# A feed-forward's tail on one Trainium2 core: the second norm of tile zero brought forward, its transposes put between the last products

## The chip, the cores and the metric

The kernel runs on one core of one Trainium2 chip. Five engines work side by side and meet only at semaphores: PE (TensorE, matrix products and transposes), DVE (VectorE), ACT (ScalarE), POOL (GpSimd) and SP (SyncE, which here only starts transfers). PE writes to PSUM, eight banks of 128 rows by 512 fp32 columns. The metric is the device time of one execution in microseconds (us); lower is better. Three runs of the kernel before took 904.01, 907.29 and 907.97 us, so its time is 907.29 us, the median.

## The reference, cut to what matters

Two transformer blocks run one after the other on 256 tokens of width 1024, all in fp32. The first ends with a feed-forward and a layer norm. The second puts 16 learned tokens (meta tokens) in front, norms the 272 rows again and multiplies them by a wide input matrix; mixing, routing and 32 experts follow.

```
h = x * (1.0 + sc2) + sh2
f = square(relu(h @ w_ff1)) @ w_ff2
x = layer_norm(ALPHA * x + gt2 * f, ln2_g, ln2_b)           # end of block one
...
h = layer_norm_2(concat([meta, x]), ln_emb_g, ln_emb_b)     # start of block two
proj = h @ w_in        # dn_qkv, dn_z, dn_b, dn_a, sb_qkv, gates
```

The change is at the seam: two layer norms in a row on the same rows, with the last feed-forward products before them and the first products of `w_in` behind them.

## The kernel before, in words

The 256 tokens are two tiles of 128, tile zero and tile one. `X[:, t, :]` holds a tile with tokens on the partitions; `hT` holds the same values with features on the partitions, as eight slices k of 128 features, which is the form that a product takes as its operand. Going from `X` to `hT` takes eight PE transposes into two PSUM banks (`transposes`, line 2184; banks 0 and 1 for tile zero, 2 and 3 for tile one) and eight evacuations that also apply the gain and the bias of the second norm (`features` on ACT, line 2514; for tile one DVE does four of the eight, `to_hT`, line 2682).

Every engine's program is written out by hand in one fixed order, with waits on semaphores. There is no scheduler: what stands later on an engine waits for what stands earlier.

The second feed-forward product is done in a form with seven products for eight (numbered 1 to 7, each summing 16 steps j in the PSUM bank of its own number; `ff2`, line 2466). The last work of this stage on PE is product 7 for j = 8 to 15 and then product 4 for j = 8 to 15. In the trace each fp32 product is two instructions. Each product raises the semaphore `yh` at j = 15; the fifth gives tile zero its last part, product 7 one half of tile one, and product 4 (`yh` = 9) the other half.

DVE takes the parts up: `ffn_out(t, half, ...)` is four instructions on 512 columns (sum, gate, residual, statistics; lines 2955 to 2958), `ffn_moments` one, `normalise(3, t)` the first norm (reciprocal, lines 2673 and 2675), and `second_norm(t)` the second (two statistics on line 2661, line 2663, a square root by ACT on line 2509, a reciprocal, line 2670). Before the change DVE's order is: tile zero's two halves, its first norm, one half of tile one (with the sum of line 2981), the second norm of tile zero, the other half of tile one, and its two norms. Each norm raises `xn`; `xn_count(i, t)` says how often it must have been raised.

`pe_second` is PE's program for block two. Before the change it begins with the transposes of tile zero, then a product on tile zero's `hT` (the value part of `sb_qkv` for tile zero, line 496, 8 products of 512 columns into bank 6; it waits for `hT0`, which ACT raises after slices 0 to 3 and again after 4 to 7), then the transposes of tile one, then `pe_side(0)`: the first quarter of the product that gives z (line 471, 8 products of 256 columns into bank 7, on tile zero only). The product on line 504 (`dn_b` and `dn_a`, all 272 rows) is the first that needs tile one's `hT`. Behind it line 520 runs 22 groups of products on all rows.

The weights come through a ring of five slots that SP fills; a slot is filled again when PE has raised `used` for what was in it.

Of the kernel before, what the change touches and what calls it, by code (L numbers as in the profile page):

```python
# [15 lines left out]
KD = DM // P  # L16
# [170 lines left out]
def build(nc, IN, out):  # L187

    ctx = ExitStack()
    with ctx:  # L190
# [15 lines left out]
        S = namedtuple("Semaphores", names)(*[ctx.enter_context(nc.semaphore("s_" + n)) for n in names])  # L206
# [22 lines left out]
        def V(name, a=0, b=None):  # L229
            o, k = COLS[name]  # L230
            return col[:, o + a:o + (k if b is None else b)]
# [121 lines left out]
        def xn_count(i, t):  # L353

            return 6 + 2 * t + i - 4 if i in (3, 4) else 2 * (i - 1) + t + 1
# [101 lines left out]
            else:  # L457
                eng.wait_ge(S.g2_mm, side_before + 3 * (i // 4) + i % 4 + 1)

        def pe_side(pe, mm, i):  # L460
            n = AT["dn_z"] + i // 4
            if i % 4 == 0:
                landed_wait(pe, n)
            earlier = [j for j in range(i) if SIDE_BANK[j] == SIDE_BANK[i]]
            if earlier:
                pe.wait_ge(S.side_ev, earlier[-1] + 1)
            w = ring_at(n).rearrange("p (k n) -> p k n", k=KD)
            o = psum[:, SIDE_BANK[i], 0:NT]
            for k in range(KD):
                if i < 4:  # L470
                    last = mm(o, hT[:, k, tok(i // 2)], w[:, k, (i % 2) * NT:(i % 2 + 1) * NT],
                              start=(k == 0), stop=(k == KD - 1))
                else:
                    last = mm(o, w[:, k, (i % 4) * P:(i % 4 + 1) * P], hT[:, k, META:L2],  # L474
                              start=(k == 0), stop=(k == KD - 1))
            last.then_inc(S.used if i % 4 == 3 else S.g2_mm, 1)

        def act_side(act, i):
            side_wait(act, i)
# [7 lines left out]

        def pe_second(pe, mm, transposes, out_proj, keep_warm):
            tr = nc.tensor.transpose
            transposes(4, 0, 1)  # L490
            landed_wait(pe, AT["sb_qkv"] + 2)
            w = ring_at(AT["sb_qkv"] + 2).rearrange("p (k n) -> p k n", k=KD)
            for k in range(KD):
                if k % 4 == 0:
                    pe.wait_ge(S.hT0, k // 4 + 1)
                last = mm(b_(6), hT[:, k, tok(0)], w[:, k, :], start=(k == 0), stop=(k == KD - 1))
            last.then_inc(S.g2_mm, 1)
            transposes(4, 1)
            pe_side(pe, mm, 0)
            pe.wait_ge(S.hT, 4)  # L500

            pe.wait_ge(S.in_dn, 48)
            for k in range(KD):
                last = mm(psum[0:8, 4, 0:L2], wba[:, k, :], hT[:, k, :], start=(k == 0), stop=(k == KD - 1))
            last.then_inc(S.ba_mm, 1)
            for g, (n, m, form) in enumerate(GROUPS):
# [5 lines left out]
                for k in range(KD):  # L512
                    if form == 2:
                        for j in range(4):
                            last = mm(psum[32 * j:32 * j + 32, g % 4, 0:P].rearrange("p (a d) -> p a d", a=2),
                                      hT[:, k, 0:32],
                                      w[:, k, :].rearrange("p (a h d) -> p a h d", a=2, h=4)[:, :, j, :],
                                      start=(k == 0), stop=(k == KD - 1))
                    elif form == "T":
                        last = mm(psum[:, g % 4, 0:L2], w[:, k, m * P:(m + 1) * P], hT[:, k, :],  # L520
                                  start=(k == 0), stop=(k == KD - 1))
                    else:
                        last = mm(psum[:, g % 4, :], hT[:, k, tok(form)], w[:, k, :],
                                  start=(k == 0), stop=(k == KD - 1))
                last.then_inc(S.used if ends_chunk(g) else S.g2_mm, 1)
                if g == 0:
                    pe.wait_ge(S.ba_ev, 1)
                    for t in range(3):
                        last = tr(psum[0:(META if t == 2 else P), 5, 8 * t:8 * t + 8], baT[:, tok(t)],
                                  C("ident")[0:8, 0:8])  # L530
# [22 lines left out]
            for t, b in enumerate((3, 7, 4)):  # L553
# [4 lines left out]
                for h in range(DH):  # L558
                    last = tr(psum[0:(META if t == 2 else P), b, h * P:(h + 1) * P], cv[:, 8 + h, tok(t)], C("ident"))
# [3 lines left out]
            for t in range(3):  # L563
                for h in range(DH):
                    last = tr(psum[0:(META if t == 2 else P), t, h * P:(h + 1) * P], cv[:, 4 + h, tok(t)], C("ident"))
# [19 lines left out]
            for p in range(12):  # L585
                last = tr(bank_prob(0, p, 2), prob(M2, p), C("ident") if p < 8 else C("ident")[0:META, 0:META])
# [52 lines left out]
            for h in range(DH):  # L639
                last = mm(psum[0:META, 5, h * P:(h + 1) * P], prob(M6, 8 + h), vb[0:META, 2, h * P:(h + 1) * P],  # L640
                          start=True, stop=True)
# [6 lines left out]
            for p in range(8):  # L648
                last = mm(psum[LOW, 3, 64 * p:64 * p + 64], prob(M4, p)[LOW, LOW], prob(M5, p)[LOW, LOW],
                          start=True, stop=True)  # L650
            last.then_inc(S.rd_mm, 1)
            pe.wait_ge(S.uv, 1)
            for h in range(DH):
                last = mm(psum[:, 2, h * P:(h + 1) * P], kdec[0:META, 2, h * P:(h + 1) * P],
                          M2[0:META, h * P:(h + 1) * P], start=True, stop=True)
# [4 lines left out]
            for p in range(8):  # L660
                last = mm(psum[LOW, 4, 64 * p:64 * p + 64], prob(M3, p)[HIGH, LOW], prob(M6, p)[HIGH, HIGH],
                          start=True, stop=True)
# [5 lines left out]
            for p in range(8):  # L668
                f = slice(64 * p, 64 * p + 64)
                last = mm(psum[LOW, 3, f], T1n[:, f], Yc[:, f], start=True, stop=True)  # L670
# [116 lines left out]
            for h in range(DH):  # L787
                last = mm(psum[:, 0, h * P:(h + 1) * P], kdec[:, 0, h * P:(h + 1) * P], M4[:, h * P:(h + 1) * P],
                          start=True, stop=True)
# [1375 lines left out]
        def _(pe):  # L2165
# [282 lines left out]
            def ff2(j, products):  # L2448

                n = ff2_chunk(j // 2)
                landed_wait(pe, n)
                pe.wait_ge(S.ff_st, j + 1)
                w = ring_at(n).rearrange("p (m n) -> p m n", m=4)
                a = [fTr[:, (2 * j + k) % 16, :] for k in range(2)]
                b = [w[:, 2 * (j % 2) + k, :] for k in range(2)]
                S1, S2, S3, S4 = SK[:, j % 2, 0, :], SK[:, j % 2, 1, :], SK3[:, j % 8, :], SK[:, j % 2, 2, :]  # L2460
                T1, T2, T3, T4 = TWK[j % 2][0], TWK[j % 2][1], TK[:, j % 8, 0, :], TK[:, j % 8, 1, :]
                for i in products:
                    lhsT, rhs = {1: (a[0][:, 0:P], b[0][:, 0:512]), 2: (a[1][:, 0:P], b[1][:, 0:512]),
                                 3: (S4, b[1][:, 512:DM]), 4: (a[1][:, P:NT], T4),
                                 5: (S1, T1), 6: (S2, T2), 7: (S3, T3)}[i]
                    last = mm(b_(i), lhsT, rhs, start=(j == 0), stop=(j == FT // 2 - 1))  # L2466
                    if j == FT // 2 - 1:
                        last.then_inc(S.yh, 1)
                return last
# [19 lines left out]
            ff2(15, (1, 6, 5, 3, 2))  # L2489
            for i in (7, 4):  # L2490
                for j in range(8, 16):
                    last = ff2(j, (i,))
                    if i == 7 and j == 8:
                        last.then_inc(S.used, 1)
# [4 lines left out]
        def _(act):  # L2499
# [7 lines left out]
            def ln_sqrt(i, t):  # L2507
                act.wait_ge(S.ln_v, ln_count(i, t))
                nc.scalar.activation(sd[:, t:t + 1], mv[:, t, 1:2], ACT.Sqrt, bias=epsc).then_inc(S.ln_s, 1)

            def features(i, t, ks, A1, B1):
                act.wait_ge(S.xn_tr, tr_count(i, t))
                for k in ks:
                    last = nc.scalar.activation(hT[:, k, tok(t)],
                                                psum[:, 2 * t + k // 4, (k % 4) * P:(k % 4 + 1) * P],
                                                ACT.Identity, bias=B1[:, k:k + 1], scale=A1[:, k:k + 1])
                return last
# [119 lines left out]
            ln_sqrt(3, 0)  # L2637
            ln_sqrt(4, 0)
            features(3, 0, range(4), V("ge"), V("be")).then_inc(S.hT0, 1)
            ln_sqrt(3, 1)  # L2640
            features(3, 0, range(4, KD), V("ge"), V("be")).then_inc(S.hT0, 1)
            ln_sqrt(4, 1)
            features(3, 1, range(4, KD), V("ge"), V("be")).then_inc(S.hT, 1)
            act_second(act, link, ln_sqrt, act_hT)
# [3 lines left out]
        def _(dve):  # L2648
# [16 lines left out]
            def normalise(i, t, rows=None):  # L2665

                dve.wait_ge(S.ln_s, ln_count(i, t))
                link(v.reciprocal(rstd[:, t:t + 1], sd[:, t:t + 1]))
                if rows is None:
                    v.tensor_scalar(X[:, t, :], X[:, t, :], mv[:, t, 0:1], rstd[:, t:t + 1],  # L2670
                                    ALU.subtract, ALU.mult).then_inc(S.xn, 1)
                else:
                    link(v.scalar_tensor_tensor(X[:, t, :], X[:, t, :], mv[:, t, 0:1], rows[:, 0, :],
                                                ALU.subtract, ALU.mult))
                    v.scalar_tensor_tensor(X[:, t, :], X[:, t, :], rstd[:, t:t + 1], rows[:, 1, :],
                                           ALU.mult, ALU.add).then_inc(S.xn, 1)
# [286 lines left out]
            def second_norm(t):  # L2963
                dve.wait_ge(S.xn, xn_count(3, t))
                moments(4, t)
                normalise(4, t)
# [10 lines left out]
            link(ffn_out(0, 0, p1s, 2))  # L2977
            ffn_moments(0)
            normalise(3, 0, rowB[:, 0])
            dve.wait_ge(S.yh, 8)  # L2980
            v.tensor_tensor(u3s, u2s, b_(7), ALU.add)
            ffn_out(1, 1, vs, 7)
            second_norm(0)
            dve.wait_ge(S.yh, 9)
            link(ffn_out(1, 0, u3s, 4))
            ffn_moments(1)
# [104 lines left out]
```

## Time and profile before

| | |
|---|---|
| runs (median, lowest, highest) | 907.29, 904.01, 907.97 us |
| profiled execution | 907.25 us |
| its span, from first to last instruction | 905.4 us |
| mean granted TensorE clock | 0.989 of full speed |
| PE busy | 867.8 us (96% of the span) |
| DVE, ACT, POOL busy | 361.7, 180.5, 93.1 us |
| the stretch of the change | 348 to 381 us |

Rows of the trace are instructions of one engine that were merged where they follow each other: start, duration of the row, engine, line, operation, output <- inputs, count, and in square brackets how long the engine had been idle before and what ended that. PE's instructions overlap in its pipeline, so a row's duration is a little longer than the time after which the next can start; the rows of the chain of waits (the work that ended last, followed back) have that overlap taken off. PEclk is the clock that was granted to TensorE, as a share of full speed.

### The profile page before, as it was taken

Reading aid. Unit: us, or ns where it says so; the run is one execution under the profiler, and the core shown is the slowest. Engines: PE = TensorE matmul, PEld = TensorE weight load, DVE = VectorE, ACT = ScalarE, POOL = GpSimd, SP = SyncE. Lnnn points to the kernel's source line nnn. Section 1 sums busy time; section 2 is a strip of 40 time slices with the busy share of each in tenths; the row PEclk is TensorE's granted clock in tenths of the full one; section 3 lists DMA queues with packets and bytes.
Section 4 is the critical chain, followed back from the end, with each engine's and each line's share of the span. In section 5 each row is a group of like instructions: output and inputs, shape, how many; then the busy total and the mean of one; then the engine's idle time right before and its main releaser. Section 6 shows DMA issues by size and latency. Waiting matters only on the chain.

```text
span 905.4 us, 11803 instructions
## 1 busy us (share of the span) xinstructions
PE 867.8 (96%) x4825; PEld 546.4 (60%) x4825; DVE 361.7 (40%) x826; ACT 180.5 (20%) x368; POOL 93.1 (10%) x91
## 2 busy tenths in 40 slices
PE   6999899999999999899999999999989999999994
PEld 3446757766667774588868888877455333333331
DVE  5735846533223338465094523533264111101014
ACT  4126512100000000322323224530111111001001
POOL 0034242401011110300000000000200000000000
PEclk9999999999999999999999999999989999999998
DMA  9997776643334446024343222024969999999993
GB/s 366 429 420 285 295 310 245 266 186 147 123 128 172 185 187 266 1 93 143 136 168 112 95 94 94 9 93 146 427 263 321 372 402 425 419 422 422 418 416 139
DMA packets 24653, 218.29 MB, mean 241 GB/s; under 512 B 3658, under 2 KB 3938, under 8 KB 10003
## 3 DMA queue, kind: packets, MB, share of 16 engines
q1 hardware_dynamic: 21330, 205.76, 57.0%
q0 software_dynamic: 3264, 11.72, 3.5%
q8 instruction: 40, 0.66, 0.3%
q14 instruction: 19, 0.15, 0.0%
HBM read 218.65 MB, written 2.10 MB: 244 GB/s over the span
## 4 chain that ended last, share of the span: by engine, by line
PE 90%; DVE 5%; ACT 2%; issue 1%; DMA 1%; SPq 0%; DVEq 0%; ACTq 0%
PE psum L2444 12%; PE psum L2466 9%; PE psum L1462 9%; PE psum L520 8%; PE psum L474 6%; PE psum L2225 6%; PE psum L1517 4%; PE psum L1486 4%; PE psum L803 3%; PE psum L2417 3%; PE psum L2199 3%; PE psum L2170 3%; PE psum L597 2%; PE psum L1440 1%; DMA ring<-in_stream 1%
## 5 line engine op out<-in xcount | busy, mean ns | idle before, releaser
L2444 PE MATMUL psum<-hT,ring 128*128 128x256 f32 x512 | 115.3, 379 | 0.0
L2444 PEld LDWEIGHTS psum<-hT,ring 128*128 128x128 f32 x512 | 97.1, 190 | 24.8 <-issue 13.1
L520 PE MATMUL psum<-hT,ring 128*128 128x272 f32 x320 | 74.2, 393 | 0.0
L520 PEld LDWEIGHTS psum<-hT,ring 128*128 128x128 f32 x320 | 60.6, 190 | 12.9 <-issue 0.5
L2466 PE MATMUL psum<-scr 128*128 128x512 f32 x128 | 59.5, 592 | 0.0
L2928 DVE TENSOR_TENSOR scr<-ring 128x512 f32<-128x512 f32 x16 | 11.1, 691 | 119.4 <-PE psum L2466 119.4
L474 PE MATMUL psum<-hT,ring 128*128 128x256 f32 x256 | 58.6, 383 | 0.0
L1462 PE MATMUL psum<-ring,hT 128*32 128x512 f32 (+1 forms) x240 | 56.5, 594 | 0.1
L2225 PE MATMUL psum<-ring,hT 128*128 128x512 f32 (+1 forms) x128 | 54.2, 586 | 2.1 <-ACT hT L2538 2.1
L1462 PE MATMUL psum<-scr,hT 128*64 128x512 f32 (+1 forms) x192 | 51.6, 614 | 2.2 <-issue 2.2
L1871 DVE TENSOR_TENSOR scr<-psum,scr 128x256 f32<-128x256 f32 x11 | 4.7, 425 | 119.6 <-ACT scr L1631 119.6
L474 PEld LDWEIGHTS psum<-hT,ring 128*128 128x128 f32 x256 | 47.5, 190 | 7.0 <-issue 0.6
L2466 PE MATMUL psum<-ring,scr 128*128 128x512 f32 x96 | 46.2, 592 | 0.0
L2633 ACT ACTIVATE scr<-psum 128x256 f32<-128x256 f32 x32 | 12.3, 383 | 168.7 <-PE psum L2444 168.7
L2225 PEld LDWEIGHTS psum<-ring,hT 128*128 128x128 f32 x128 | 24.9, 195 | 31.0 <-issue 31.0
L2466 PEld LDWEIGHTS psum<-scr 128*128 128x128 f32 x128 | 24.3, 190 | 24.6 <-issue 23.9
L2158 POOL TENSOR_TENSOR scr<-scr 128x256 f32<-128x256 f32 x32 | 20.6, 644 | 154.5 <-ACT scr L2633 154.5
L1486 PE MATMUL psum<-rowB,scr 128*128 128x512 f32 x80 | 36.3, 596 | 0.0
L2170 PE MATMUL psum<-cst 128*128 128x512 f32 x66 | 31.7, 627 | 0.0
L1462 PEld LDWEIGHTS psum<-ring,hT 128*32 128x32 f32 (+1 forms) x240 | 16.1, 119 | 23.1 <-issue 22.4
L803 PE MATMUL psum<-scr,ring 128*128 128x256 f32 x128 | 29.0, 382 | 0.0
L1462 PEld LDWEIGHTS psum<-scr,hT 128*64 128x64 f32 (+1 forms) x192 | 14.7, 129 | 23.2 <-issue 23.2
(579 smaller groups left out, 1271.3 us busy)
## 6 DMA issues: line engine op xcount, KB each, us to landing
ring<-in_stream SPq DMA_DIRECT2D x54, 2048.0 KB, 9.4
ring<-in_gates SPq DMA_DIRECT2D x9, 2048.0 KB, 21.6
ring<-in_downs SPq DMA_DIRECT2D x14, 1024.0 KB, 21.8
scr<-in_gates SPq DMA_DIRECT2D x6, 2048.0 KB, 26.8
scr<-in_gates SPq DMA_DIRECT2D x8, 1024.0 KB, 29.0
scr<-in_downs SPq DMA_DIRECT2D x8, 1024.0 KB, 15.4
scr<-in_stream SPq DMA_DIRECT2D x3, 2048.0 KB, 19.1
rowB<-in_rows POOLq DMA_DIRECT2D x5, 1024.0 KB, 12.1
```

Source lines behind the costliest of these rows:

```text
L474: last = mm(o, w[:, k, (i % 4) * P:(i % 4 + 1) * P], hT[:, k, META:L2], start=(k == 0), stop=(k == KD - 1))
L520: last = mm(psum[:, g % 4, 0:L2], w[:, k, m * P:(m + 1) * P], hT[:, k, :], start=(k == 0), stop=(k == KD - 1))
L803: last = mm(o, w[:, k, m * P:(m + 1) * P], src[:, k, :], start=(k == 0), stop=(k == 3))
L1462: last = mm(psum[i * w:(i + 1) * w, 2, :], xg[p % 2][:, k, i * w:(i + 1) * w], block_of(GATE[e], k), start=(k == 0), stop=(k == KD - 1))
L1486: last = mm(b_(4 + 2 * t + half), scat[p % 2][:, t * P:(t + 1) * P], yg[:, half * 512:(half + 1) * 512], start=(p == 0), stop=False)
L1517: last = mm(psum[i * w:(i + 1) * w, half, :], turned[p % 2][:, c:c + w], block_of(DOWN[e], 4 * (e % 2) + 2 * half + f), start=(f == 0), st ...
L2170: mm(psum[:, bank, 0:width], C("ident"), C("neg").broadcast_to([P, width]), start=True, stop=True)
L2199: last = mm(b_(4 + 2 * t + half), src[:, k, t * P:(t + 1) * P], w[:, k, :], start=(k == 0), stop=(k == KD - 1))
L2225: return mm(psum[:, 2 * c + t, 0:b - a], hT[:, k, tok(t)], ring_at(AT["head"] + k)[:, 2048 + a:2048 + b], start=(k == 0), stop=(k == KD - 1))
L2417: last = mm(o, mixT[:, k, t * P:(t + 1) * P], w[:, k, cols], start=(k == 4), stop=(k == 3))
L2444: last = mm(psum[:, f if f < 4 else 0, 0:NT], w[:, k, m * P:(m + 1) * P], hT[:, k, META:L2], start=(k == order[0]), stop=(k == order[-1]))
L2466: last = mm(b_(i), lhsT, rhs, start=(j == 0), stop=(j == FT // 2 - 1))
```

## The change

Four pieces move. On DVE, `second_norm(0)` goes from behind the first half of tile one to directly behind the first norm of tile zero. On PE, `transposes(4, 0, 1)` (tile zero) goes from the head of `pe_second` to in front of product 4's last two steps, j = 14 and 15. On PE, the z quarter is cut in two: slices 0 to 3 before the transposes of tile one, slices 4 to 7 behind them, with a new wait for `xn` (first norm of tile one) ahead of the first half. On ACT, the square root of tile one's first norm goes behind the second four evacuations of tile zero. No instruction is added or removed.

PE at the end of the feed-forward (line numbers in the changed kernel are a few higher: 2468 is 2466, 2186 is 2184). Before:

```order
L2466 MATMUL psum<-scr 128x512 x16
L2184 MATMUL psum<-cst,X 128x128 x8
L496 MATMUL psum<-ring,hT 128x512 x8
L2184 MATMUL psum<-cst,X 128x128 x8
L471 MATMUL psum<-ring,hT 128x256 x8
```

And now:

```order
L2468 MATMUL psum<-scr 128x512 x14
L2186 MATMUL psum<-cst,X 128x128 x8
L2468 MATMUL psum<-scr 128x512 x2
L496 MATMUL psum<-ring,hT 128x512 x8
L471 MATMUL psum<-ring,hT 128x256 x4
L2186 MATMUL psum<-cst,X 128x128 x8
L471 MATMUL psum<-ring,hT 128x256 x4
```

Tile zero's eight transposes now stand ahead of the last two products, and tile one's stand in the middle of the z quarter.

DVE from the last instruction of tile zero's first norm on (2675, now 2679) to the first instruction that needs product 4. Before:

```order
L2675 SCALAR_TENSOR_TENSOR X<-X,small,rowB 128x1024
L2981 TENSOR_TENSOR scr<-scr,psum 128x512
L2955 TENSOR_TENSOR scr<-scr,psum 128x512
L2956 TENSOR_TENSOR scr<-scr 128x512
L2957 SCALAR_TENSOR_TENSOR X<-X,scr 128x512
L2958 BN_STATS small<-X 128x6
L2661 BN_STATS small<-X 128x6 x2
L2663 BN_AGGR small<-small 128x2
L2668 RECIPROCAL small<-small 128x1
L2670 TENSOR_SCALAR X<-X,small 128x1024
L2955 TENSOR_TENSOR scr<-scr,psum 128x512
```

And now:

```order
L2679 SCALAR_TENSOR_TENSOR X<-X,small,rowB 128x1024
L2665 BN_STATS small<-X 128x6 x2
L2667 BN_AGGR small<-small 128x2
L2672 RECIPROCAL small<-small 128x1
L2674 TENSOR_SCALAR X<-X,small 128x1024
L2986 TENSOR_TENSOR scr<-scr,psum 128x512
L2959 TENSOR_TENSOR scr<-scr,psum 128x512
L2960 TENSOR_TENSOR scr<-scr 128x512
L2961 SCALAR_TENSOR_TENSOR X<-X,scr 128x512
L2962 BN_STATS small<-X 128x6
L2959 TENSOR_TENSOR scr<-scr,psum 128x512
```

The four instructions of the second norm have changed places with the five of tile one's first half. The diff:

```
-        def pe_side(pe, mm, i):
+        def pe_side(pe, mm, i, ks=range(KD)):
...
-            for k in range(KD):
+            for k in ks:
                 if i < 4:
                     last = mm(o, hT[:, k, tok(i // 2)], w[:, k, (i % 2) * NT:(i % 2 + 1) * NT],
                               start=(k == 0), stop=(k == KD - 1))
...
-            last.then_inc(S.used if i % 4 == 3 else S.g2_mm, 1)
+            if KD - 1 in ks:
+                last.then_inc(S.used if i % 4 == 3 else S.g2_mm, 1)
...
         def pe_second(pe, mm, transposes, out_proj, keep_warm):
             tr = nc.tensor.transpose
-            transposes(4, 0, 1)
             landed_wait(pe, AT["sb_qkv"] + 2)
...
             last.then_inc(S.g2_mm, 1)
+            pe.wait_ge(S.xn, xn_count(3, 1))
+            pe_side(pe, mm, 0, range(4))
             transposes(4, 1)
-            pe_side(pe, mm, 0)
+            pe_side(pe, mm, 0, range(4, KD))
             pe.wait_ge(S.hT, 4)
...
             for i in (7, 4):
                 for j in range(8, 16):
+                    if i == 4 and j == 14:
+                        transposes(4, 0, 1)
                     last = ff2(j, (i,))
...
             features(3, 0, range(4), V("ge"), V("be")).then_inc(S.hT0, 1)
+            features(3, 0, range(4, KD), V("ge"), V("be")).then_inc(S.hT0, 1)
             ln_sqrt(3, 1)
-            features(3, 0, range(4, KD), V("ge"), V("be")).then_inc(S.hT0, 1)
             ln_sqrt(4, 1)
...
             normalise(3, 0, rowB[:, 0])
+            second_norm(0)
             dve.wait_ge(S.yh, 8)
             v.tensor_tensor(u3s, u2s, b_(7), ALU.add)
             ffn_out(1, 1, vs, 7)
-            second_norm(0)
             dve.wait_ge(S.yh, 9)
```

## Rows read from the trace of the kernel before

**Rows 1.** The page: the span, and each engine's busy time

```profile
span 905.4 us, 11803 instructions
PE 867.8 (96%) x4825; PEld 546.4 (60%) x4825; DVE 361.7 (40%) x826; ACT 180.5 (20%) x368; POOL 93.1 (10%) x91
```

**Rows 2.** Chain of waits in order of time: start, duration, what

```profile
363.18 1.11 PE psum L2184 x8
364.31 1.51 ACT hT L2514 x4
...
373.06 0.87 PE psum L2184 x8
373.93 3.46 PE psum L471 x16
...
385.26 58.86 PE psum L520 x256
```

**Rows 3.** Timeline of PE across the seam

```profile
348.48 13.90 PE L2466 MATMUL psum<-scr 128*128 128x512 f32 x32
...
363.18 1.09 PE L2184 MATMUL psum<-cst,X 128*128 128x128 f32 x8 [0.80 <-DVE X L2670]
...
365.95 7.11 PE L496 MATMUL psum<-ring,hT 128*128 128x512 f32 x16 [1.69 <-ACT hT L2514]
...
377.32 3.83 PE L504 MATMUL psum<-hT,sm 128*8 128x272 f32 x16
```

**Rows 4.** The page's groups: line 2466, busy and mean ns

```profile
L2466 PE MATMUL psum<-scr 128*128 128x512 f32 x128 | 59.5, 592 | 0.0
```

**Rows 5.** Timeline of DVE in the same stretch

```profile
355.65 1.28 DVE L2675 SCALAR_TENSOR_TENSOR X<-X,small,rowB 128x1024 f32<-128x1024 f32 x1
356.86 0.68 DVE L2981 TENSOR_TENSOR scr<-scr,psum 128x512 f32<-128x512 f32 x1
...
360.23 1.27 DVE L2661 BATCH_NORM_STATS2 small<-X 128x6 f32<-128x512 f32 x2
...
362.31 0.81 DVE L2670 TENSOR_SCALAR X<-X,small 128x1024 f32<-128x1024 f32 x1
363.04 0.68 DVE L2955 TENSOR_TENSOR scr<-scr,psum 128x512 f32<-128x512 f32 x1
...
368.02 1.28 DVE L2675 SCALAR_TENSOR_TENSOR X<-X,small,rowB 128x1024 f32<-128x1024 f32 x1
...
371.43 0.81 DVE L2670 TENSOR_SCALAR X<-X,small 128x1024 f32<-128x1024 f32 x1
```

**Rows 6.** Timeline of ACT in the same stretch

```profile
361.78 0.29 ACT L2509 ACTIVATE small<-small 128x1 f32<-128x1 f32 x1 [7.68 <-DVE small L2663]
...
366.17 0.29 ACT L2509 ACTIVATE small<-small 128x1 f32<-128x1 f32 x1 [0.36 <-DVE small L2961]
...
373.97 1.50 ACT L2514 ACTIVATE hT<-psum,col 128x128 f32<-128x128 f32 x4 [2.77 <-PE psum L2184]
...
375.97 1.28 ACT L482 ACT_TABLE_LOAD   x1
```

**Rows 7.** Windows: PE, PEld, DVE, ACT, POOL busy, clock, DMA share, GB/s

```profile
360.00:375.00 15.00, 12.52 (x44) 6.69 (x43) 11.81 (x23) 4.80 (x14) 0.92 (x1) 1.00 0.00 0
...
670.00:680.00 10.00, 9.24 (x33) 6.48 (x34) 5.75 (x30) 0.30 (x2) 0.00 (x0) 0.55 0.18 73
...
720.00:760.00 40.00, 39.98 (x219) 14.89 (x216) 7.02 (x15) 4.40 (x9) 2.97 (x3) 1.00 1.00 407
760.00:800.00 40.00, 37.74 (x195) 14.49 (x195) 5.73 (x11) 5.05 (x9) 1.98 (x2) 0.96 1.02 422
```

**Rows 8.** Waits of SP's transfer queue from 560 us on

```profile
SPq L2010 <- DVE perm L1732: 18.6, 1, 18.6
```

**Rows 9.** Timeline of PE in the experts

```profile
779.67 8.78 PE L1462 MATMUL psum<-scr,hT 128*64 128x512 f32 x32 [2.24 <-issue]
```

**Rows 10.** Chain of waits later on, same line and count

```profile
829.17 7.02 PE psum L1462 x32
```

More of the change, by code:

```diff
@@ L458, in side_wait, with pe_side @@
                 eng.wait_ge(S.g2_mm, side_before + 3 * (i // 4) + i % 4 + 1)
-        def pe_side(pe, mm, i):
+        def pe_side(pe, mm, i, ks=range(KD)):
             n = AT["dn_z"] + i // 4
@@ L468, in pe_side @@
             o = psum[:, SIDE_BANK[i], 0:NT]
-            for k in range(KD):
+            for k in ks:
                 if i < 4:
@@ L475, in pe_side @@
                               start=(k == 0), stop=(k == KD - 1))
-            last.then_inc(S.used if i % 4 == 3 else S.g2_mm, 1)
+            if KD - 1 in ks:
+                last.then_inc(S.used if i % 4 == 3 else S.g2_mm, 1)
         def act_side(act, i):
@@ L489, in pe_second @@
             tr = nc.tensor.transpose
-            transposes(4, 0, 1)
             landed_wait(pe, AT["sb_qkv"] + 2)
@@ L497, in pe_second @@
             last.then_inc(S.g2_mm, 1)
+            pe.wait_ge(S.xn, xn_count(3, 1))
+            pe_side(pe, mm, 0, range(4))
             transposes(4, 1)
-            pe_side(pe, mm, 0)
+            pe_side(pe, mm, 0, range(4, KD))
             pe.wait_ge(S.hT, 4)
@@ L2491, in _ @@
                 for j in range(8, 16):
+                    if i == 4 and j == 14:
+                        transposes(4, 0, 1)
                     last = ff2(j, (i,))
@@ L2639, in _ @@
             features(3, 0, range(4), V("ge"), V("be")).then_inc(S.hT0, 1)
+            features(3, 0, range(4, KD), V("ge"), V("be")).then_inc(S.hT0, 1)
             ln_sqrt(3, 1)
-            features(3, 0, range(4, KD), V("ge"), V("be")).then_inc(S.hT0, 1)
             ln_sqrt(4, 1)
@@ L2979, in _ @@
             normalise(3, 0, rowB[:, 0])
+            second_norm(0)
             dve.wait_ge(S.yh, 8)
@@ L2982, in _ @@
             ffn_out(1, 1, vs, 7)
-            second_norm(0)
             dve.wait_ge(S.yh, 9)
```

## The prediction

> **What bounds the kernel now.** I read the page first: PE is busy 867.8 of 905.4 us [rows 1], so this is a kernel bound by PE, and time can only be won where PE stands idle or works slowly. The chain of waits comes next: across the seam it leaves PE for DVE and ACT and comes back, and behind it runs on PE in one piece, as in the 58.86 us of line 520 [rows 2]. So the seam is a place where PE waits for somebody. The timeline of PE says how long: 0.80 us before the transposes of tile zero (for line 2670, the last step of its second norm) and 1.69 us before line 496 (for ACT's first four evacuations) [rows 3]. Together 2.49 us of 905.4, 0.3%. Timelines of DVE and ACT then say when each operand is ready [rows 5, 6], and the windows that the clock granted here is 1.00 and that no transfer runs [rows 7].
>
> **Step 1: tile zero's second norm.** DVE ends line 2675 at 355.65 + 1.28 = 356.93. Before, five instructions of tile one come first, from 356.86 to 360.23, 3.37 us, and the second norm takes from 360.23 to 362.31 + 0.81 = 363.12, 2.89 us with ACT's square root in it [rows 5]. Moved ahead, it runs from about 356.97 to 359.86. The five instructions follow, until 359.86 + 3.37 = 363.23 less the overlap of about 0.07 that rows 5 show between neighbours (2675 ends at 356.93, 2981 starts at 356.86): about 363.2.
>
> **Step 2: the transposes between the products.** The last 32 instructions of line 2466 take 13.90 us, each lasts 0.592 [rows 3, 4]; so one starts every (13.90 - 0.592) / 31 = 0.429 us. Product 4's j = 14 starts at 348.48 + 28 x 0.429 = 360.50. The operand is there at 359.86, so the transposes wait for nothing, with 0.64 us to spare. Eight of them take 0.87 us net [rows 2], and push j = 14 and 15 back by that: product 4, which ended at 348.48 + 13.90 = 362.38 [rows 3], ends at 363.25. A wait is added in front of these products, so this margin counts: behind it stand four product instructions, and for them DVE's second half of tile one.
>
> The Trainium skill, "TensorE: Matmul & The Clock Gate", section "Back-to-back issue gap", gives some 81 ns for each 128-column matmul in a sustained stream with weight loads; by that figure the eight would take an estimated 0.65 us, and the gain would come out about 0.1 us larger. The trace has 0.87 us, 109 ns each, and the sum goes by that.
>
> **Step 3: line 496.** ACT's four evacuations start when the transposes' last result is there, 1.09 us after their start [rows 3] and about 0.04 later, and take 1.51; PE starts 0.13 behind, as 365.82 to 365.95 [rows 2, 3]: 360.50 + 1.09 + 0.04 + 1.51 + 0.13 = 363.27. PE itself is free at 360.50 + 0.87 + 4 x 0.429 = 363.09. So line 496 starts at 363.27 where it started at 365.95 [rows 3]: 2.68 us earlier. The stall of 1.69 us shrinks to 0.2, because four product instructions, 1.72 us, now lie over ACT's work.
>
> **Step 4: tile one, which is late next.** DVE can take the last part at 363.2 by its own work and at 363.25 + 0.04 by PE's: 363.29 instead of 363.04, 0.25 us later. From there to the end of tile one's second norm DVE needs what it needed, 371.43 + 0.81 - 363.04 = 9.20 us [rows 5], so the operand of tile one's transposes is ready at 372.49 instead of 372.24. ACT's reordering costs nothing: its eight evacuations of tile zero end near 361.6 + 3.0 = 364.6, and the square root that now stands behind them is wanted at about 366.17 + 0.25 [rows 6], so 1.8 us cover it; without that cover it would add 1 for 1.
>
> **Step 5: the z quarter as filler.** Line 496's 16 instructions take 16 x 0.429 = 6.87, until 370.14. The new wait for tile one's first norm is met at 368.02 + 1.28 + 0.25 = 369.55 [rows 5], 0.6 us before. If it were not, nothing is lost but filler: behind it on PE stand half the z quarter and tile one's transposes, and these wait for a later norm anyway. Half of line 471, 3.46 / 2 = 1.73 [rows 2], fills PE until 371.87. Then PE waits for the operand until 372.49 + 0.06 (as 363.12 to 363.18 [rows 3, 5]) = 372.55, 0.68 us idle. Without the cut it would have idled 2.4 us.
>
> **Step 6: where the gain is handed on.** Tile one's transposes start at 372.55. PE goes on with 0.87 + 1.73 until 375.15. ACT and DVE end tile one's `hT` at 372.55 + 1.09 + 0.04 + 1.50 = 375.18 [rows 3, 6], and PE starts line 504 behind it at 375.18 + 0.13 = 375.31. Before it started at 377.32 [rows 3], held by its own queue and not by `hT`, which was ready near 375.47 [rows 6]. The sum is 377.32 - 375.31 = 2.01 us, 2.0. What was a chain on PE (transposes and a whole z quarter behind tile one's norm) has become a chain DVE, PE, ACT; tile one's norm is the next limit, and it did not move.
>
> **Does it reach the end?** Behind line 504 PE works without a hole for 58.86 us and more [rows 2]; ACT's table load and DVE's small work that lie there [rows 6] take their turn from PE's results and move along. No transfer hangs on the moved instructions: none runs from 360 to 375 [rows 7], and the next slots are released by line 520. The experts stream at 407 to 422 GB/s [rows 7] and could hold the end in place, but that stream is started by DVE's routing result (18.6 us of SP's waiting [rows 8]), in a stretch where the DMA share is 0.18 [rows 7]; it moves along too.
>
> **The sum.** The profiled execution took 907.25 us, 905.4 of span and 1.85 around it, and stands 0.04 under the median of the runs, so no correction: 907.25 - 2.0 = 905.25, say 905.3. Bounds: PE without any hole from 360.50 to tile one's transposes (0.87 + 1.72 + 6.87 + 1.73) and 2.76 us of evacuation and restart behind them would start line 504 at 374.45, a gain of 2.9; with the gain lost below, 0.
>
> **The rivals.** (a) The gain is real at the seam and does not reach the end: the experts' weights arrive when they did. For it: the DMA share of 1.00 to 1.02 from 720 to 800 and the 2.24 us that PE waited at 777 us [rows 7, 9]. Against: the released start above. Then 907.0 to 907.3.
>
> (b) Slower: the second norm is not ready when PE reaches its transposes, and the two products behind them stall. The place is product 4, j = 14; each us beyond the margin of 0.64 delays product 4, tile one and line 504 by one. The 2.0 us are used up when the norm ends 2.64 us late, taking 5.5 us where it took 2.89. If it were 4 us late, 907.25 + 1.4 = 908.6. For it: the norm needs ACT in its middle. Against: ACT had been idle for 7.68 us when this square root came to it [rows 6], and DVE has nothing else in between.
>
> (c) The clock elsewhere. The granted clock fell to 0.55 on average from 670 to 680 us and to 0.96 from 760 to 800, the second time around a wait of PE for 2.24 us [rows 7, 9]; these are its two levels, 2.4 and 1.2 GHz, mixed over the window. The second spell cost line 1462 8.78 us where 32 such took 7.02 [rows 9, 10], 1.76 us. One such spell more makes 907.1, one less 903.5; one like the first, up to 4.5 us, makes 909.8 or 900.8. The Trainium skill, the same page, "Part 1: The HAM clock gate", says that the clock is halved by default and that the array's activity releases it; by that rule fewer holes at the seam can win a spell there, but the clock there is 1.00 already [rows 7], so the seam has none to win.
>
> (d) The change does not do what it says: DVE still ends tile one late and PE waits the whole gain away in front of tile one's transposes. That needs tile one's norm 2 us later than 372.49; 0.25 us is all that the rows give. Then 907.3.
>
> **How the numbers follow.** Forecast 0.72, at 905.3; (a) and (d) together 0.16, at 907.0 to 907.3; (b) 0.04, at 908.6; (c) 0.08, half to each side. The runs of before spread from 3.3 below to 0.7 above their median, and a median of a few runs moves by part of that; so the range goes from 905.3 - 2.4 to (a) and 0.6 above it, 902.9 to 907.8. About 0.5% (4.5 us) is what a measurement of this kernel can tell from no change; 2 us is less than half. Faster by more needs 902.75 or less: the spread around the forecast gives 0.05 and a lost spell of clock 0.02, 0.07. Slower by more needs 911.8: (b) and (c) at their worst, 0.03. The rest, 0.90, is no change that can be told.
>
> **What would show it.** The transposes of tile zero start at about 360.5 with no idle time and line 496 near 363.3; the idle time before line 496 falls from 1.69 to 0.2 us; a new wait of about 0.7 us for line 2670 (2674 in the changed kernel) stands before tile one's transposes; line 504 starts 2.0 us earlier, and the start of the transfers behind the routing is earlier by as much. It is wrong if the transposes between the products wait, if tile one's norm ends more than 0.5 us later, or if the 2 us are at line 504 and no longer at the end.

## The result: 902.01 us, and the profile after

The changed kernel took 902.01 us, the median of five runs (901.85 to 902.89), beside 907.29 us for the kernel before (904.01 to 908.66, five runs). The medians differ by 5.3 us; the ratio on record is 0.9948, with a 95% interval of 0.9925 to 0.9970. Forecast were 2.0 us less, and 902.9 was the lower end of the range; to 902.75 or less I had given 0.07. The direction was right, the size was not. Its profiled execution took 901.93 us, with a span of 900.1 us against 905.4 [rows 1] and a granted clock of 0.993 against 0.989.

The timeline of PE across the seam in the changed kernel, to be laid beside [rows 3] (line 2468 is 2466 of before, 2186 is 2184, 506 is 504; in the experiments below the numbers move by a few again, and a row is known by its operation and tiles):

```profile
347.78 12.18 PE L2468 MATMUL psum<-scr 128*128 128x512 f32 x28
359.79 1.04 PE L2186 MATMUL psum<-cst,X 128*128 128x128 f32 x8
360.67 1.88 PE L2468 MATMUL psum<-scr 128*128 128x512 f32 x4
362.52 7.11 PE L496 MATMUL psum<-ring,hT 128*128 128x512 f32 x16
369.46 1.89 PE L471 MATMUL psum<-ring,hT 128*128 128x256 f32 x8
371.86 1.09 PE L2186 MATMUL psum<-cst,X 128*128 128x128 f32 x8 [0.51 <-DVE X L2674]
372.79 1.89 PE L471 MATMUL psum<-ring,hT 128*128 128x256 f32 x8
374.61 3.83 PE L506 MATMUL psum<-hT,sm 128*8 128x272 f32 x16
```

The row of line 2468 starts 0.70 us earlier than in the kernel before (347.78 for 348.48), long before anything that the change touches: that belongs to this execution, not to the change. Counted from there, line 506 starts after 26.83 us and line 504 of before after 28.84. The seam gives 2.01 us. The distance hardly varies: it is 28.83 to 28.85 us in all five traces with the order of before (before, e2, e6, e8 and e13 below) and 26.83 to 26.85 in all six with the order of the change (after, e3, e5, e7, e9, e14). Both idle times of [rows 3] are gone, and one of 0.51 us is new, before tile one's transposes.

The timeline of DVE in the same stretch, beside [rows 5]:

```profile
356.27 1.29 DVE L2665 BATCH_NORM_STATS2 small<-X 128x6 f32<-128x512 f32 x2
...
358.36 0.82 DVE L2674 TENSOR_SCALAR X<-X,small 128x1024 f32<-128x1024 f32 x1
359.09 0.68 DVE L2986 TENSOR_TENSOR scr<-scr,psum 128x512 f32<-128x512 f32 x1
...
362.58 0.69 DVE L2959 TENSOR_TENSOR scr<-scr,psum 128x512 f32<-128x512 f32 x1
...
370.99 0.81 DVE L2674 TENSOR_SCALAR X<-X,small 128x1024 f32<-128x1024 f32 x1
```

Tile zero's second norm ends at 359.18 and PE's transposes start at 359.79: the spare 0.6 us are there.

So where are the other 3 us? I followed the same instructions through both traces. Up to the routing the lead stays what it was at line 506: line 1371 starts 2.72 us earlier. At the first expert product it is 5.82. The timeline of PE there, in the kernel before:

```profile
670.76 0.41 PE L1371 MATMUL psum<-scr,cst 128*128 128x32 f32 x2 [1.78 <-DVE scr L1698]
...
684.01 2.37 PE L1462 MATMUL psum<-ring,hT 128*64 128x512 f32 x10
```

and in the changed kernel (lines two higher):

```profile
668.04 0.41 PE L1373 MATMUL psum<-scr,cst 128*128 128x32 f32 x2 [1.77 <-DVE scr L1700]
...
678.19 2.37 PE L1464 MATMUL psum<-ring,hT 128*64 128x512 f32 x10
```

The same work takes 13.25 us in one and 10.15 in the other. The windows of the changed kernel (columns as in [rows 7]) say why:

```profile
660.00:670.00 10.00, 7.49 (x40) 4.81 (x39) 8.23 (x37) 3.09 (x7) 0.53 (x1) 0.97 0.87 348
670.00:680.00 10.00, 9.91 (x58) 6.44 (x59) 7.43 (x32) 1.87 (x2) 0.43 (x1) 0.86 0.40 134
```

The clock shares missing here, 0.03 and 0.14 of 10 us, make 3.4 us at 1.2 GHz; in the kernel before the share was 0.55 from 670 to 680 [rows 7], and windows of 1 us put its spell from 671.0 to 681.3, 10.2 us. In the experts a little is given back: line 1464 of the seventh group, in front of which the code waits for the group's weights, starts 5.48 us earlier, and it idles 2.69 us for 2.24 [rows 9]:

```profile
774.19 8.79 PE L1464 MATMUL psum<-scr,hT 128*64 128x512 f32 x32 [2.69 <-issue]
```

The account of the profiled pair: 0.70 (earlier work of that execution) + 2.01 (seam) + 3.10 (routing) - 0.34 (before the seventh group) - 0.2 (behind it) = 5.3 us of span. It holds for these two executions; how far it holds for the medians is what the experiments are about.

### The profile page after: what moved, and what is told of

Read it like the earlier page. It is cut to its first block, busy times and chain, and to the rows that moved or that the text cites. A ratio compares the mean times of both kernels' runs of the same rounds, so it can differ in the third digit from the quotient of the medians.

```text
span 900.1 us, 11804 instructions
## 1 busy us (share of the span) xinstructions
PE 863.6 (96%) x4825; PEld 542.8 (60%) x4825; DVE 362.1 (40%) x826; ACT 180.7 (20%) x368; POOL 93.2 (10%) x91
## 4 chain that ended last, share of the span: by engine, by line
PE 88%; DVE 6%; DMA 2%; issue 1%; ACT 1%; SPq 0%; DVEq 0%; ACTq 0%
PE psum L2446 12%; PE psum L2468 11%; PE psum L1464 9%; PE psum L522 8%; PE psum L474 6%; PE psum L1519 4%; PE psum L1488 4%; PE psum L2227 4%; PE psum L805 3%; PE psum L2419 3%; PE psum L2201 3%; PE psum L2172 3%; DMA ring<-in_stream 2%; PE psum L599 2%; PE psum L1442 1%
```

## The experiments

The theory that I started with, A: the seam gives 2.0 us, the rest is a shorter spell at the lower clock in the routing, and its length hangs on when PE gets there. Rival B: the new order of work is itself worth 5.3 us. Rival C: the spell's length is drawn anew in each run, and the runs of the result drew well. Times are medians; the kernel before was run again beside each set of kernels, on the same chip, and its median is given for each. A filler is an idle product of 512 columns on the identity, 0.86 us (`keep_warm`). "Low" counts the runs whose mean granted clock was 0.990 or less. The expectations take it for the share of long spells in the routing; only the profiled execution of each kernel can show whether it is, and a table further down does that.

| kernel | median us | runs | low | kernel before beside it |
|---|---|---|---|---|
| before, all runs of the four sets | 906.34 | 127 | 39 | |
| changed, with the result's five | 902.89 | 29 | 5 | |
| e1 changed + 2.1 us at the seam | 906.86 | 12 | 6 | 906.49 |
| e2 before + routing fillers | 904.87 | 12 | 0 | 906.49 |
| e3 changed + routing fillers | 901.92 | 6 | 0 | 906.49 |
| e4 changed, quarter undivided | 906.05 | 12 | 4 | 906.49 |
| e5 changed | 902.77 | 12 | 2 | 906.64 |
| e6 before + routing and seam fillers | 904.71 | 12 | 0 | 906.64 |
| e7 changed + routing and expert fillers | 902.33 | 12 | 0 | 906.64 |
| e8 before + divided quarter | 906.27 | 10 | 3 | 906.64 |
| e9 changed | 903.30 | 12 | 3 | 905.89 |
| e10 changed + 0.86 us at the seam | 904.21 | 12 | 2 | 905.89 |
| e11 changed + 3.43 us at the seam | 906.66 | 12 | 2 | 905.89 |
| e12 before + 2.1 us at the seam | 907.50 | 12 | 4 | 905.89 |
| e13 before + routing fillers | 904.65 | 12 | 1 | 906.01 |
| e14 changed + routing fillers | 902.88 | 11 | 0 | 906.01 |
| e15 changed + routing fillers + 2.1 us | 905.02 | 12 | 0 | 906.01 |

**Is it the order, or the time?** The changed kernel with the seam's time given back:

```
             pe.wait_ge(S.hT, 4)
+            keep_warm(4, 2)
+            keep_warm(4, 1, 192)
```

Expected of e1: 

> The changed kernel with three idle-filling products (about 2.1 us, 512, 512 and 192 columns on the identity) on PE in front of the product that first needs tile one's hT: the seam's gain of 2.0 us is given back, the order of the work stays. Theory A (2.0 us come from the seam, the other 3 us from a shorter spell at the lower clock in the routing at 670 us, and how long that spell is hangs on when PE gets there): the arrival is that of the kernel before, the spell is 10 us again, the time 906.5 to 908. Rival B (the new order itself is worth all of the 5.3 us): 904.1. Rival C (the length of the spell is drawn anew in each run, whatever the kernel): runs scattered from 904 to 908, as those of the kernel before.

Measured: 906.86, beside 906.49 for the kernel before; ratio 0.9994 (0.9977 to 1.0011). Its trace, PE at the seam and then PE and the windows at the routing:

```profile
348.58 12.18 PE L2470 MATMUL psum<-scr 128*128 128x512 f32 x28
...
375.35 2.32 PE L2174 MATMUL psum<-cst 128*128 128x512 f32 x6
377.60 3.83 PE L508 MATMUL psum<-hT,sm 128*8 128x272 f32 x16
...
671.03 0.41 PE L1375 MATMUL psum<-scr,cst 128*128 128x32 f32 x2 [1.77 <-DVE scr L1702]
...
684.28 1.94 PE L1466 MATMUL psum<-ring,hT 128*64 128x512 f32 x8
```

```profile
670.00:680.00 10.00, 8.97 (x34) 6.21 (x35) 6.12 (x31) 0.30 (x2) 0.00 (x0) 0.59 0.19 74
```

377.60 - 348.58 = 29.02 us, 0.18 more than before; the routing takes 13.25 us again, to the hundredth. With the time given back nothing is left of the gain, so B falls. The median is in the 906.5 to 908 of theory A, but the runs scatter from 904.3 to 908.7, which is what C says.

**Filling the hole in the routing.** One edit, in each of the two kernels:

```
             last.then_inc(S.lg_mm, 1)
-            keep_warm(6, 3)
+            keep_warm(6, 5)
```

Expected of e2: 

> The kernel before with two idle-filling products more (five for three, 1.72 us) in the hole of 1.78 us in which PE waits for DVE's routing, ahead of line 1371; nothing else. Theory A and rival C: the clock no longer falls there, the stretch from line 1371 to the first expert product takes 9 to 10 us for 13.25, and the time is 903 to 904. Rival B (the clock spell is not what the time comes from): 907.3, no change.

Expected of e3: 

> The changed kernel with the same two idle-filling products more in the routing. Theory A: the remaining 3.4 us at the lower clock go too, worth about 1 us: 900.5 to 901.5; and against the kernel before with the same fillers (clock equal in both) the change is worth 2.0 us and no more. Rival B: 5.3 us under that kernel, so below 899. Rival C: 2.0 us under it too.

Measured: 904.87 and 901.92, both above what was expected (903 to 904, and 900.5 to 901.5). PE in e2, and the window:

```profile
666.12 4.55 PE L2170 MATMUL psum<-cst 128*128 128x512 f32 x10
670.72 0.41 PE L1371 MATMUL psum<-scr,cst 128*128 128x32 f32 x2
...
680.31 6.23 PE L1462 MATMUL psum<-ring,hT 128*64 128x512 f32 x28
```

```profile
670.00:680.00 10.00, 9.00 (x64) 6.83 (x62) 7.12 (x31) 0.83 (x3) 0.00 (x0) 1.00 0.36 120
```

No idle time stands before line 1371, the clock is 1.00, and the stretch takes 9.59 us for 13.25. The long spell is worth 3.7 us where it comes; over the runs the fillers give the kernel before 1.6 by the medians of this set (ratio 0.9976, 0.9959 to 0.9993) and 1.4 in the last set below (e13), whose ratio, 0.9995 (0.9977 to 1.0013), is not clear of no change. The gap between the two kernels with fillers is 2.95 us here, from six runs of one of them; the last set below repeats the comparison and gives 1.8.

**The parts of the change.** e4 keeps the norm, the transposes and ACT's order and puts the z quarter back whole behind tile one's transposes; e8 puts only the divided quarter into the kernel before.

```
-            pe.wait_ge(S.xn, xn_count(3, 1))
-            pe_side(pe, mm, 0, range(4))
             transposes(4, 1)
-            pe_side(pe, mm, 0, range(4, KD))
+            pe_side(pe, mm, 0)
```

Expected of e4: 

> The changed kernel with the z quarter whole and behind tile one's transposes, as before the change; DVE's new order and tile zero's transposes between the products stay. Theory A: PE stands idle 2.4 us before tile one's transposes, and line 504 starts 0.4 us earlier than in the kernel before, for 2.0 with the split (both counted from the first instruction of products 7 and 4). The time by the seam alone 906.9; with a spell of other length in the routing 903.5 to 907. Rival (the gain at the seam is from the norm and the transposes, the split is of no account): 2 us earlier at line 504, 902 to 903.

Expected of e8: 

> The kernel before with the z quarter split around tile one's transposes and nothing else: norm, tile zero's transposes and ACT's order as before. Tile one's transposes then start behind half the quarter, at 374.5 instead of 372.9, and line 504 waits for hT: 374.55 + 1.09 + 0.04 + 1.50 + 0.13 = 377.3, where it was. No change at line 504 (0.0 us), no change in time. Rival (the split is worth something by itself): line 504 more than 0.5 us earlier.

Measured: 906.05 (ratio 0.9988, 0.9972 to 1.0004) and 906.27 (1.0001, 0.9977 to 1.0024). PE in e4, and a window:

```profile
348.15 12.18 PE L2466 MATMUL psum<-scr 128*128 128x512 f32 x28
...
372.23 1.80 PE L2184 MATMUL psum<-cst,X 128*128 128x128 f32 x8 [2.23 <-DVE X L2672]
373.82 4.63 PE L471 MATMUL psum<-ring,hT 128*128 128x256 f32 x16
378.39 3.83 PE L504 MATMUL psum<-hT,sm 128*8 128x272 f32 x16
```

```profile
370.00:380.00 10.00, 7.77 (x32) 5.82 (x33) 3.25 (x14) 3.94 (x8) 5.74 (x2) 0.83 0.00 0
```

The wait of 2.23 us is the one forecast for this order (2.4), and here the clock fell behind it: eight transposes take 1.80 us for 1.04, the quarter 4.63 for 3.62. Line 504 comes 378.39 - 348.15 = 30.24 us behind the start of the products, 1.4 later than before. In the kernel before, transposes and quarter take 4.42 us, from the row below to line 504 at 377.32 [rows 3]:

```profile
372.90 1.04 PE L2184 MATMUL psum<-cst,X 128*128 128x128 f32 x8
```

Had they taken as long in e4, line 504 would have come 0.3 us earlier than before; that is an estimate, 0.4 were expected, and no trace shows this order without the spell. PE in e8:

```profile
348.60 13.90 PE L2469 MATMUL psum<-scr 128*128 128x512 f32 x32
...
374.74 1.03 PE L2187 MATMUL psum<-cst,X 128*128 128x128 f32 x8
...
377.44 3.83 PE L507 MATMUL psum<-hT,sm 128*8 128x272 f32 x16
```

377.44 - 348.60 = 28.84, exactly the kernel before. In the traces the divided quarter alone gives nothing, the rest alone 0.3 us at an unchanged clock (the estimate above) and a loss with the spell; together they give 2.0. The medians of e4 and e8 cannot be told from the kernel before.

**The seam's holes and the clock.** e6 fills the routing and both holes of the seam in the kernel before:

```
             tr = nc.tensor.transpose
+            keep_warm(0, 1, 448)
             transposes(4, 0, 1)
+            keep_warm(6, 2)
```

Expected of e6: 

> The kernel before with two fillers more in the routing (as in the earlier run) and, in the two holes of the seam, one filler of 448 columns before tile zero's transposes and two of 512 behind them; order and waits unchanged. If the seam's holes of 0.80 and 1.69 us let the clock fall in some runs (as the hole of 2.23 us did in the kernel with the undivided quarter, where it cost 1.8 us), the median comes 0.5 to 1 us under the 904.9 of the routing fillers alone. If not: 904.9, the same, and the change's 2.0 us are waiting time alone.

Measured: 904.71, where e2 had 904.87. Holes of 0.80 and 1.69 us cost waiting time and no clock that these runs can show.

**A version meant to beat both.** e7 fills the routing and, with `if p == 6: keep_warm(2, 3)` at the head of `gate_up`, the wait before the seventh group.

Expected of e7: 

> The changed kernel with two fillers more in the routing and three fillers in the hole of 2.7 us at 771 us in the experts, ahead of the wait for the seventh group's weights. If spells of the lower clock are what scatters the runs: median 900 to 901, spread under 2 us, faster than both kernels; the spell at 774 us (32 products of line 1462 in 8.8 us) becomes 7.0. If that group then waits for its weights anyway, since the transfers are at 419 GB/s there: 901.9 as without them.

Measured: 902.33, ratio to the kernel before 0.9956 (0.9936 to 0.9975). In its trace:

```profile
771.70 2.85 PE L2174 MATMUL psum<-cst 128*128 128x512 f32 x6
774.48 7.09 PE L1466 MATMUL psum<-scr,hT 128*64 128x512 f32 x32
```

The spell there is gone, 7.09 us for 8.79. The median beside e3's and e14's shows no gain from it, and 900 to 901 was missed. The traces show where such a gain goes. In e14 (the changed kernel with routing fillers alone, below) the clock happened not to fall in this place:

```profile
773.55 7.09 PE L1464 MATMUL psum<-scr,hT 128*64 128x512 f32 x32 [2.00 <-issue]
...
874.55 0.62 PE L1464 MATMUL psum<-ring,hT 128*32 128x512 f32 x1 [1.36 <-DMA scr<-in_gates]
```

PE then waits 1.36 us for the weights of the last group, as it does in e7 (1.36 us) and in e2 (1.12), which have no spell either; in the traces before and after, which have one, it does not wait there. From the start of the seventh group to the end of the span it is 125.9 us both in e14 and in after, 125.4 in e2 and 125.7 in before. So this spell costs 1.7 us at its place and at most 0.3 at the end of these traces: the weights hold the end, as the second branch of the expectation had it, only at the last group and not at the seventh. With the routing fillers alone the changed kernel had 901.92 and 902.88, without them 902.89 over 29 runs: e7 and the changed kernel with routing fillers are 3.1 to 4.6 us better than the kernel before beside them, and not distinguishable from the changed kernel.

**Drawn or tied to the arrival?** The changed kernel again, twice; then with other delays (`keep_warm(4, 1)`, `keep_warm(4, 4)` where e1 has its fillers); and e1's fillers in the kernel before.

Expected of e5: 

> The changed kernel itself, once more, with more runs beside more runs of the kernel before. Theory C (2.0 us from the seam; the spells at the lower clock in the routing and the experts differ from run to run and the five runs of the result had short ones by chance): median 904 to 905 with a spread of some 4 us, 2.0 to 2.5 us under the kernel before. Theory A (spells tied to the time of arrival): 902 again, all runs within 1 us, 4.5 us under it.

Expected of e9: 

> The changed kernel a third time, for the share of its runs with a long spell at the lower clock (mean granted clock of the run at 0.990 or less). So far 2 of 17 runs, and 26 of 64 of the kernel before. Theory A (the share hangs on when PE gets to the routing): again about 1 in 8, median 902 to 903. Theory C (same share for every arrival, the 2 of 17 were chance): 4 to 5 of 12, median 904 to 905.

Expected of e10: 

> The changed kernel with one filler of 512 columns (0.86 us) in front of line 506: PE gets to the routing 1.15 us earlier than in the kernel before. Theory A: share of long spells between the two, 2 to 4 of 12, median 904. Theory C: as the other kernels, 5 of 12, median 905. The 0.86 us are given back in both.

Expected of e11: 

> The changed kernel with four fillers of 512 columns (3.43 us) there: PE gets to the routing 1.4 us later than in the kernel before. If the share of long spells follows the arrival and not the order of work, it differs from the 6 of 12 that the kernel with 2.1 us of fillers had. The time without any difference in the spells: 902.8 + 3.4 = 906.2; with the spells of the kernel before 908.

Expected of e12: 

> The kernel before with the fillers of 2.1 us in front of line 504, the ones that the first experiment put into the changed kernel. Theory C: 906.6 + 2.1 = 908.7, share of long spells 5 of 12. Theory A: another share, in either direction, and the time between 907 and 910.

Measured: 902.77 (ratio 0.9962, 0.9944 to 0.9979) and 903.30 (0.9970, 0.9956 to 0.9984) for the changed kernel, with single runs up to 906.55. The 5.3 us came back as 3.9 and 2.6. Over all runs the gap is 3.45 in medians, 3.5 +- 0.6 in means. Neither theory came out clean. Against A: the changed kernel had 3 low runs of 12 in the set where the kernel before had 8 of 35. For it: over all sets the share is 5 of 29 against 39 of 127, kernels that reach the routing when the kernel before does (e1, e8) had 9 of 22, and the one that comes 1.4 us later (e11) 2 of 12, its median being the changed kernel's plus 3.77 for 3.43 us of fillers, while e1's is that plus 3.97 for 2.1. e10 (904.21, 2 low of 12) came out as A says, and e12 (907.50, 4 of 12) 1.2 under C's 908.7, with 1.6 over the kernel before beside it for 2.1 us of fillers. These counts are too small to settle it.

The profiled executions show the spells themselves. These are all ten without fillers in the routing, in the order in which PE starts the line that is 1371 in before; the times at which the clock fell are from the trace's record of the granted clock:

| trace | line 1371 at, us | clock falls, us from that start | spell, us | line 1371 to first expert product | mean clock |
|---|---|---|---|---|---|
| after | 668.04 | 1.3 behind | 3.4 | 10.15 | 0.993 |
| e5 (changed) | 668.70 | not | 0 | 9.59 | 0.993 |
| e9 (changed) | 670.28 | not | 0 | 9.58 | 0.993 |
| before | 670.76 | 0.3 behind | 10.2 | 13.25 | 0.989 |
| e8 | 670.87 | 0.8 behind | 10.2 | 13.24 | 0.987 |
| e1 | 671.03 | 0.7 behind | 10.2 | 13.25 | 0.988 |
| e10 | 671.29 | 4.1 ahead | 3.4 | 9.59 | 0.991 |
| e4 | 671.82 | 1.0 behind | 3.4 | 10.10 | 0.989 |
| e11 | 672.38 | 1.9 behind | 3.4 | 10.09 | 0.994 |
| e12 | 672.61 | 4.0 ahead | 3.4 | 9.59 | 0.990 |

Three things can be read. One and the same kernel had a spell in one execution and none in two others (after; e5 and e9), so the spell does differ from run to run. The three long spells are those where the clock fell within 0.8 us behind the start of line 1371, and also those where that line starts between 670.7 and 671.1; with one trace of most kernels the two cannot be told apart, so A is neither shown nor ruled out. And a low mean clock is not a long spell in the routing: e4 and e12 have the one without the other. The window of e5, to be laid beside those of the changed kernel above:

```profile
670.00:680.00 10.00, 8.96 (x61) 6.46 (x62) 7.70 (x34) 1.87 (x2) 0.33 (x1) 1.00 0.44 146
```

Nor do the routing's spells account for all of the scatter. e9's profiled execution took 905.77 us without any spell in the routing, 3.9 us of span more than after's: 2.2 us of that were lost before the first row of the seam (350.02 for 347.78, at a clock of 1.00 in both traces), 2.2 between the first expert product and the end, and 0.6 won back in the routing. And the two kernels' runs above 0.990 still differ by 2.8 +- 0.5 us in means (in medians 902.78 over 24 runs of the changed kernel and 905.50 over 88 of the kernel before).

**The seam with the routing pinned, on one chip.**

Expected of e13: 

> The kernel before with two fillers more in the routing, on one chip with the two kernels below: no run at 0.990 or less, median 904.9.

Expected of e14: 

> The changed kernel with the same two fillers. With the routing's clock level in both, the gap to the kernel above is the seam's 2.0 us if nothing else is in the change: median 902.9. If the order of work gives more than the seam shows: 2.5 to 3, median 902.2.

Expected of e15: 

> The changed kernel with the two routing fillers and, as in the first experiment, 2.1 us of fillers in front of line 506. Only the seam's gain counts: 904.9 to 905.0, as the kernel before with the routing fillers. If the order gives 0.5 us or more beside the seam: 904.4 or less.

Measured: 904.65, 902.88 and 905.02. One run of e13 was at 0.990, where none was expected, and two more of its runs took 907.29 and 910.75 us at 0.997 and 0.993, so that no low clock goes with them. The gap of the first two is 1.8 us; with e2 and e3 it is 2.01 in medians (24 runs against 17), 2.4 +- 1.0 in means. Giving 2.1 us back brings the changed kernel to 905.02, 0.4 above the first. With the hole in the routing filled the change is worth the seam's 2.0 us, and nothing more that these runs can show; up to 1.3 us more lies within their noise.

## Why the prediction was right at the seam and wrong in the sum

Each step of the seam came as forecast. Less the 0.70 us by which that execution was early, the forecast end of tile zero's second norm was 359.16 and it ended at 359.18; the transposes were to start at 359.80 and started at 359.79 without waiting; product 4 ended at 362.55, as forecast; line 496 was to start at 362.57 and did at 362.52; tile one's operand, forecast for 371.79, was there at 371.80; the new idle time before its transposes is 0.51 us for 0.68; line 506 was to start at 374.61 and did. The 0.2 us of idle time that were to be left before line 496 did not come. Rivals (b) and (d) did not happen. The step "Does it reach the end?" held: line 1371 has the whole lead of 2.7 us, and with the routing filled in both kernels the 2.0 us are there in the median at the end, so rival (a) fell too. (The side estimate of Step 2, a gain 0.1 us larger with shorter transposes, counts only tile zero's in the changed kernel; counted for both tiles and both kernels it comes out about 0.1 us smaller, also an estimate. Nothing rests on it.)

What failed is rival (c), the clock elsewhere. I gave it 0.04 to the faster side and 0 in the sum, as if the routing's spell in the trace before were a fixed cost that both kernels carry. It is a cost that differs between executions: 10.2 us at 1.2 GHz in the profiled one of the kernel before, 3.4 in the first of the changed kernel, none in its two others. That term measured 3.1 us in the profiled pair. Over all runs what is left beside the seam is about 1.5 (3.5 less 2.0), and 0 to 0.4 with the hole filled. Rival (c) had its second price wrong as well: 1.76 us for a spell in the experts, which is worth 0.3 at most at the end of the traces (e14 beside after, e2 beside before), since PE without it waits for weights. I had the sign that it could go (the runs before spread over 4 us, the granted clock of the page was one draw) and used the spread only as noise around a median of three.

The second size was that median. 907.29 was the level of three runs, later of five; 127 runs put it at 906.34. And the changed kernel's five runs were at the low end of its own: 902.01, where 29 runs give 902.89. Of the 5.28 us measured, 2.0 are the seam, 1.8 the luck of the two samples (907.29 - 906.34 and 902.89 - 902.01), and about 1.5 are left. That the seam is worth 2.0 is shown, by the traces and by e13 to e15 together with e1. That the 1.5 are the routing's spells is likely and not shown: the fillers there give the kernel before 1.7 us in medians (906.34 to 904.65) and the changed one 0.3 (902.89 to 902.64), but the gap of 3.5 +- 0.6 without them and that of 2.4 +- 1.0 with them overlap, and the runs above 0.990 differ by 2.8. Whether the changed kernel draws fewer long spells, and why, stays open.

## What to carry to other kernels

Filling a wait and making its operand ready earlier can be worth something only together: here 0.3 (an estimate) and 0.0 us apart, 2.0 together. Worked through by the arrival of every operand, this stretch came out within 0.05 us of the forecast at six points; but look in the same trace for spells of low clock behind a wait, since here they differed from run to run and the long one, 3.7 us, was larger than the gain. Where a few us matter, fill such a hole in both kernels first and compare those, and do not take a median of three as the level. And before a spell is priced, see what waits behind it: in the experts the weights took its price away.

## What the runs showed of the hardware that was not expected

Around a hole of only 1.78 us the clock fell to 1.2 GHz for 3.4 us in some traces, for 10.2 in others and not at all in two; PE was busy all through the long spell (9.24 of 10 us from 670 to 680 [rows 7], its idle part being ahead of line 1371). In two traces with the short spell (e10, e12) the clock fell some 4 us ahead of line 1371, while PE ran idle products, and the slower products covered the hole: there the spell cost nothing, 9.59 us to the first expert product as with no spell at all. Two fillers, 1.72 us, in that hole took the low runs of the kernel before from 39 of 127 to 1 of 36 (e2, e6, e13); with all kernels that have them it is 1 of 77. A hole of 2.23 us at the seam let the clock fall too in the one trace that has such a hole (e4); holes of 0.80 and 1.69 did not in any of the traces. The length of a hole alone does not decide: ahead of the seventh group holes of 2.00, 2.06 and 2.59 us passed without a fall (e14, e11, e2), while one of 2.04 (e1) did not.
